# The first expert item picked by 0/1 matmuls, the last item combined by a matmul, the first norm taken over token rows, and the query and key norms packed in 16 rows

## The reference, cut to what matters

```
# layer 0
h = rmsnorm(x, norm_mix_even)                   # mean of squares over the 1024 channels of a token
a, gate, q, k, v = split(h @ w_in)
c = silu(layernorm(causal_depthwise_conv(a * sigmoid(gate))))     # 31 taps
q, k = rmsnorm(q per head of 64), rmsnorm(k per head of 64)       # 8 heads each
o = stick_breaking(q, k, v)                     # the samples also over 256 cached keys and values
x = x + concat(c, o) @ w_out;  x = x + swiglu(rmsnorm(x))
# layer 1
x = x + retention(rmsnorm(x))
h = rmsnorm(x, norm_ffn_odd)
top_val, top_idx = top_k(h @ router_w, 2);  gates = softmax(top_val)
x = x + sum over e of combine[:, e] * ((silu(h @ w_gate[e]) * (h @ w_up[e])) @ w_down[e])   # 8 experts, each token in 2
```

## Time and profile before

| | us |
|---|---|
| median of 3 runs (1799.4 to 1803.44) | 1800.45 |
| the profiled execution's own time | 1801.37 |
| its span in the trace | 1799.6 |
| PE busy | 1677.4 (93% of the span) |
| DVE busy | 1293.9 (72%) |
| ACT busy | 1049.5 (58%) |
| POOL busy | 71.2 (4%) |

### The profile page before, as it was taken

One profiled execution on the slowest core, in us unless ns is written; L12 is line 12 of the kernel. 1 busy time (PEld: TensorE's weight loads), 2 busy tenths in 40 slices (PEclk: granted clock), 3 DMA queues, 4 the chain that ended last, 5 costly groups with the idle time before them and its releaser, 6 DMA issues.

```text
span 1799.6 us, 24257 instructions
## 1 busy us (share of the span) xinstructions
PE 1677.4 (93%) x9295; PEld 1446.3 (80%) x9295; DVE 1293.9 (72%) x1091; ACT 1049.5 (58%) x913; POOL 71.2 (4%) x94
## 2 busy tenths in 40 slices
PE   4986989999899998939999999999999999999995
PEld 3964989999899987928878878878788788787884
DVE  4796255544964366348888888888888888888885
ACT  3534244433342265237787777777877877868773
POOL 2014000000001000010000000000000000000001
PEclk9998699999998799969999999999999999999998
DMA  6525049755557332639999999999999999999992
GB/s 232 193 74 166 1 135 371 254 176 176 186 189 249 126 106 82 223 131 365 369 351 395 364 357 386 351 378 379 351 393 363 359 392 357 360 383 354 386 368 98
DMA packets 236652, 491.69 MB, mean 273 GB/s; under 512 B 8665, under 2 KB 66137, under 8 KB 236328
## 3 DMA queue, kind: packets, MB, share of 16 engines
q1 hardware_dynamic: 227088, 456.60, 70.6%
q0 software_dynamic: 9504, 34.24, 5.8%
HBM read 463.87 MB, written 27.42 MB: 273 GB/s over the span
## 4 chain that ended last, share of the span: by engine, by line
issue 56%; PE 33%; DVE 7%; ACT 2%; DMA 1%; POOL 0%; POOLq 0%; SPq 0%; DVEq 0%; ACTq 0%
PE bank L624 8%; PE bank L625 8%; PE bank L626 8%; PE bank L910 2%; PE bank L847 1%; DVE WL L1482 1%; DVE even_CA L1541 1%; PE bank L744 1%; DVE RS L1556 1%; DMA R<-in_param 1%; PE bank L898 1%; ACT WH L1153 1%; PE bank L1006 1%; PE bank L981 0%; PE bank L884 0%
## 5 line engine op out<-in xcount | busy, mean ns | idle before, releaser
L1847 DVE TENSOR_TENSOR WL<-moe_MORE,WH 128x2048 fp32r<-128x2048 f32 x192 | 439.3, 2291 | 86.2 <-ACT WH L1410 85.7
L1410 ACT ACTIVATE WH<-moe_MORE 128x2048 fp32r<-128x2048 f32 x192 | 368.4, 1923 | 149.6 <-PE bank L626 149.5
L1847 DVE TENSOR_TENSOR WL<-ring,WH 128x2048 fp32r<-128x2048 f32 x144 | 329.2, 2291 | 56.8 <-ACT WH L1410 55.5
L624 PE MATMUL bank<-WH,moe_XEH 128*128 128x512 f32 x896 | 360.3, 402 | 3.0 <-DVE moe_XEL L1853 2.3
L626 PE MATMUL bank<-WH,moe_XEL 128*128 128x512 f32 x896 | 354.5, 396 | 0.0
L625 PE MATMUL bank<-WL,moe_XEH 128*128 128x512 f32 x896 | 354.3, 395 | 0.0
L1410 ACT ACTIVATE WH<-ring 128x2048 fp32r<-128x2048 f32 x144 | 275.9, 1919 | 85.4 <-PE bank L626 85.4
L624 PE MATMUL bank<-HH,WH 128*128 128x264 f32 x960 | 283.9, 296 | 19.3 <-DVE HL L1500 18.2
L1482 DVE TENSOR_TENSOR WL<-ring,WH 128x2048 fp32r<-128x2048 f32 x80 | 181.0, 2264 | 140.0 <-ACT WH L1153 139.8
L625 PE MATMUL bank<-HL,WH 128*128 128x264 f32 x960 | 278.7, 290 | 0.0
L626 PE MATMUL bank<-HH,WL 128*128 128x264 f32 x960 | 278.2, 290 | 0.0
(11 more groups left out here) (296 smaller groups left out, 1850.9 us busy)
## 6 DMA issues: line engine op xcount, KB each, us to landing
moe_MORE<-in_moe_w_gate SPq DMA_DIRECT2D x72, 1024.0 KB, 6.3
moe_MORE<-in_moe_w_up SPq DMA_DIRECT2D x72, 1024.0 KB, 6.5
ring<-in_moe_w_down SPq DMA_DIRECT2D x64, 1024.0 KB, 6.7
moe_MORE<-in_moe_w_down SPq DMA_DIRECT2D x48, 1024.0 KB, 5.8
ring<-in_moe_w_gate SPq DMA_DIRECT2D x40, 1024.0 KB, 5.6
ring<-in_moe_w_up SPq DMA_DIRECT2D x40, 1024.0 KB, 6.7
ring<-in_w_in_odd SPq DMA_DIRECT2D x24, 1024.0 KB, 5.4
ring<-in_ffn_w_gate SPq DMA_DIRECT2D x11, 1024.0 KB, 8.2
```

Of the source, the lines that this page charges most:

```text
L624: mm(out, lh, rh, start=start, stop=False)
L1410: func(WH[:, q % WRING, :], chunk(q), ACT.Copy).then_inc(s_hi, 1)
L1847: V.tensor_tensor(WL[:, q % WRING, :], chunk(q), full(WH[:, q % WRING, :]), ALU.subtract)\
```

## The change

Four parts, and the waits that go with them:

1. **Start.** The first 128 token rows and only the identity and epsilon of `C` are loaded first, then the other rows and `R`, then two chunks, then the rest of `C`. ACT squares the rows as they lie (a sum for each token), DVE multiplies each row by its reciprocal root (`XN`), PE turns these to channels, ACT takes gain and rounding in one step from PSUM and DVE the rest, and PE begins chunk 0. The turns of the plain rows for `XT` come behind chunk 0.
2. **Query and key norms.** Eight matmuls with a 0/1 table sum the squares of all 16 heads into 16 rows, between the projections; one root and one reciprocal of 16 x 264 follow, the latter inside DVE's convolution loop; `SPREAD`, made by POOL, brings each row back to its 64 partitions by a matmul, and DVE multiplies from PSUM.
3. **First item.** DVE writes 0/1 tables `OH` (token by slot); 24 matmuls of `HX` by them give the turned tile of item 0, without the trip through memory. Two weight chunks are split earlier on ACT and DVE, one inside the squares. ACT also keeps the residual as rows, `XR`.
4. **Last item.** It is not written. POOL gathers the rows of the other items while the last one is computed (a row of the last item is read as zero), multiplies them by the gates and adds them and `XR`: 12 TENSOR_TENSORs of 1024 columns. At the end PE multiplies `YE` by a table `GT` of gates, token by slot, and DVE adds. 4 small transfers to `moe_pad` fill up the count of a semaphore, and two more 512 KB tiles are zeroed in the feed-forward stage.

```
# SP, start
-            sp.dma_start(XI[:, 0:2, :], x_prompt.rearrange("o (a p) d -> p (o a) d", p=P)).then_inc(s_x, 16)
-            sp.dma_start(XI[0:NS, 2, :], x_sample.rearrange("b o d -> (b o) d")).then_inc(s_x, 16)
-            sp.dma_start(C[:], const).then_inc(s_const, 16)
-            sp.dma_start(R[:], param).then_inc(s_const, 16)
+            sp.dma_start(XI[:, 0, :], x_prompt[0, 0:P, :]).then_inc(s_x0, 16)
+            sp.dma_start(C[:, 0:P + 1], const[:, 0:P + 1]).then_inc(s_x0, 16)
+            sp.dma_start(XI[:, 1, :], x_prompt[0, P:SEQ, :]).then_inc(s_x, 16)
+            sp.dma_start(XI[0:NS, 2, :], x_sample.rearrange("b o d -> (b o) d")).then_inc(s_x, 16)
+            sp.dma_start(R[:], param).then_inc(s_x, 16)
+            load_in(q, w_in_even[0], starts[0])
+            load_in(q + 1, w_in_even[0], starts[1])
+            sp.dma_start(C[:, P + 1:NCONST], const[:, P + 1:NCONST]).then_inc(s_const, 16)
# DVE, query and key norms
             for n in range(2 * HP):
-                dve.wait_ge(s_qrt, n + 1)
-                link(V.reciprocal(RS[:, n % 2, :], RS[:, n % 2, :]))
+                dve.wait_ge(s_qms, n + 2)
                 V.scalar_tensor_tensor(out=QN[:, n, :], in0=QR[:, n, :], scalar=param_("q_g" if n < HP else "k_g"),
-                                       in1=RS[:, n % 2, :], op0=ALU.mult, op1=ALU.mult).then_inc(s_qn, 1)
+                                       in1=PB[6 + n % 2][:, 0:T], op0=ALU.mult, op1=ALU.mult).then_inc(s_qn, 1)
# PE, first item
+            pe.wait_ge(s_oh, 1)
+            pe.wait_ge(s_hx, 2 * NT)
+            for k in range(DK):
+                for t in range(NT):
+                    last = mm(PB[2 if k < 4 else 7][:, (k % 4) * P:(k % 4 + 1) * P],
+                              HX[0:TOK[t], t, k * P:(k + 1) * P], OH[0:TOK[t], t, :],
+                              start=(t == 0), stop=(t == NT - 1))
+            last.then_inc(s_xtp, 1)
-            pe.wait_ge(s_hx, 2 * NT)
-            turn_in(0)
# POOL, last item
-            pool.wait_ge(s_ylast, 16)
+            pool.wait_ge(s_last, 1)
+            pool.wait_ge(s_rows, 16 * 2 * NT)
+            pool.wait_ge(s_yst, N_FILL + 16 * (MAXI - 1))
...
+            for t in range(NT):
+                y0, y1 = YO[rows, t, :], SPARE[t][rows, :]
+                pool.wait_ge(s_gy[t], 32)
+                for c, y in enumerate((y0, y1)):
+                    nc.gpsimd.tensor_tensor(y, y, GE[rows, t, 2 + c:3 + c].to_broadcast([TOK[t], D]), ALU.mult)\
+                        .then_inc(s_pre, 1)
+                pool.wait_ge(s_pre, 4 * t + 2)
+                nc.gpsimd.tensor_tensor(y0, y0, y1, ALU.add).then_inc(s_pre, 1)
+                pool.wait_ge(s_pre, 4 * t + 3)
+                nc.gpsimd.tensor_tensor(y0, y0, XR[t][rows, :], ALU.add).then_inc(s_pre, 1)
# PE, end
+            for half in range(2):
+                pe.wait_ge(s_yee, n_items * 2 + (1 + half))
+                for t in range(NT):
+                    mm(PB[back_bank(half, t)][0:TOK[t], :], GT[:, t * P:t * P + TOK[t]],
+                       YE[:, half * 512:(half + 1) * 512], start=True, stop=True).then_inc(s_turn, 1)
```

More of the change, by code:

```diff
@@ L113, in build @@
         XT = sb("XT", [P, DK, T])
-        HH = sb("HH", [P, DK, T], F32R)
-        HL = sb("HL", [P, DK, T], F32R)
+        rows_at = -(-nc.sbuf_base // 32) * 32
+        sb("rows", [P, 2 * DK * T])
+        HH = nc.alloc_sbuf_tensor_at("HH", [P, DK, T], F32R, offset=rows_at)
+        HL = nc.alloc_sbuf_tensor_at("HL", [P, DK, T], F32R, offset=rows_at + 4 * DK * T)
+        SPARE = [nc.alloc_sbuf_tensor_at(f"SPARE{i}", [P, D], F32, offset=rows_at + 2 * i * DK * T) for i in range(4)]
         SQ = sb("SQ", [P, DK, T])
@@ L684, in down, with turn_tokens @@
                         q += 1
-            pe.wait_ge(s_x, 32)
-            pe.wait_ge(s_const, 32)
+            def turn_tokens(x, k):
+                for t in range(NT):
+                    last = turn(PB[4 + k % 4][:, t * P:t * P + TOK[t]],
+                                x[0:TOK[t], t, k * P:(k + 1) * P], ident[0:TOK[t], 0:TOK[t]])
+                last.then_inc(s_turn, 1)
+            pe.wait_ge(s_x0, 32)
+            pe.wait_ge(s_ht, NT)
+            for k in range(4):
+                turn_tokens(XN, k)
+            arrived(C_EVEN)
+            wh, wl = (as_in(x) for x in parts(C_EVEN))
+            for k in range(DK):
+                pe.wait_ge(s_hl, k + 1)
+                for j in range(2):
+                    cols = slice(j * P, (j + 1) * P)
+                    last = mm3(PB[j][:, 0:T], wh[:, k, cols], wl[:, k, cols], HH[:, k, :], HL[:, k, :],
+                               k == 0, k == DK - 1)
+                    if k == DK - 1:
+                        last.then_inc(s_ag, 1)
+                if k + 4 < DK:
+                    turn_tokens(XN, k + 4)
             for k in range(DK):
@@ L691, in _ @@
                     pe.wait_ge(s_xt, k - 3)
-                for t in range(NT):
-                    last = turn(PB[k % 4][:, t * P:t * P + TOK[t]],
-                                XI[0:TOK[t], t, k * P:(k + 1) * P], ident[0:TOK[t], 0:TOK[t]])
-                last.then_inc(s_turn, 1)
+                turn_tokens(XI, k)
+            pe.wait_ge(s_xt, DK)
             pe.wait_ge(s_cc, 32)
@@ L719, in _ @@
                 project(C_EVEN + 8 + n // 2, n % 2, PB[n][:, 0:T], s_vp)
+                if n == 0:
+                    pe.wait_ge(s_qks, 2 * HP)
+                    for i in range(2 * HP):
+                        last = mm(PB[6][0:2 * H, 0:T], heads[:, 2 * H - 2 - 2 * i:4 * H - 2 - 2 * i], SQ[:, i, :],
+                                  start=(i == 0), stop=(i == 2 * HP - 1))
+                    last.then_inc(s_qms, 1)
             pe.wait_ge(s_vfe, HP)
@@ L786, in _ @@
             pe.wait_ge(s_uo, 2)
[L787 removed]
+            pe.wait_ge(s_qn, 2 * HP)
             pe.wait_ge(s_qse, 1)
@@ L1824, in _ @@
             V.tensor_copy(DX[:, :], DF[:, :]).then_inc(s_dest, 1)
+            slots = PB[3][:, 0:P]
+            for t in range(NT):
+                last = V.tensor_scalar(OH[:, t, :], slots, DF[:, t:t + 1], None, ALU.is_equal)
+            link(last)
+            for t in range(NT):
+                last = V.scalar_tensor_tensor(out=OH[:, t, :], in0=slots, scalar=DF[:, NT + t:NT + t + 1],
+                                              in1=OH[:, t, :], op0=ALU.is_equal, op1=ALU.add)
+            last.then_inc(s_oh, 1)
             rows_hx(1)
```

295 lines of the change are left out of this document (188 added, 107 removed).

## The result

The changed kernel took 1793.41 us (median of 5, 1792.15 to 1794.62) against 1800.96 for the kernel before (5, 1799.4 to 1803.44): ratio 0.996, interval 0.9946 to 0.9975. It is 7.6 us faster, less than the forecast (1780) and outside its range (1763 to 1790). A second measurement of the same two kernels gave 1797.62 (12 executions, 1789.14 to 1804.0) against 1800.39, ratio 0.9985, 0.9966 to 1.0004.

What follows compares the result with a forecast made beforehand. TensorE was busy 93% of the span, so only PE's waits or slow stretches could be won. Terms: -8.0 - 2.0 - 11.2 - 13.4 + 14 = -20.6 us, giving 1780 for the median, range 1763 to 1790.

Steps and rivals of the forecast that it cites:

- A: Start: PE begins chunk 0 16.3 us earlier, less new turns and DVE work, a gain of 8.0 us (3.7 to 11).
- B: Query and key norms: one reciprocal in DVE's loop instead of eight behind it, a gain of 2.0 us (0.5 to 3.5).
- C: Head of the expert stage: item 0 picked by matmul begins 9.6 us earlier and at full clock, gain 11.2 us.
- D: End: from PE's last matmul to the span's end 9.8 us instead of 23.3, a gain of 13.4 us.
- E: Last item: POOL's 12 operations delay DVE's rests by 1.4 us each, a loss of 14 us (0 to 18).
- 21 passes slow and 27 fast, 8.3 us: Head of the expert stage: 48 gather passes, slow ones at 0.24 us and fast ones at 0.12, 8.3 us in all.
- Item 0 at full clock: Head of the expert stage: item 0 starts at full clock, saving the 1.7 us its first ten matmuls lost.
- all passes slow: Head of the expert stage, lower bound: the passes take 11.5 us and item 0 loses again, gain 6.3 us.
- the eight matmuls lie in projections for which DVE's loop leaves room: Norms: the eight 0/1 matmuls are hidden in the projections; without DVE's loop they would cost 1.9 us.
- the 1.5 given back: Last item: DVE's operations that read PSUM can lie beside POOL, taking about 1.5 us off a loss of 15.5.
- the first rival: Last item: POOL's operations cost nothing, total gain 34.6 us, time 1766; chance 0.19.
- the second rival: Start: chunk 0 lands at 23.6 as before, so the start gives 0.4 us, time 1788; chance 0.14.

Runs made afterwards that it cites:

- e9: Changed kernel with its first item again loaded through memory, without 0/1 tables and their matmuls: 1796.01 us, ratio 0.9973 to the kernel before.
- e5: Changed kernel with the norms of queries and keys done as before, for each tile: 1798.25 us, ratio 0.9992 to the kernel before.
- f2: Changed kernel with the three edits of f1 plus the old norms (e5) and the unread matmuls (e3): 1768.48 us, ratio 0.9817 to the kernel before.
- e2: Changed kernel with the root behind the projections and the reciprocal at the end of DVE's convolution loop: 1800.02 us, ratio 0.9991 to the kernel before.
- e4: Changed kernel with POOL's early copy and first cached keys held until weight chunk 0 has landed: 1791.82 us, ratio 0.9949 to the kernel before.
- f1: Changed kernel with the edits of e4, e6 and e7 together: 1771.0 us, ratio 0.9848 to the kernel before.
- e1: Changed kernel without POOL's twelve products and sums, its six gathers kept: 1778.89 us, ratio 0.9884 to the kernel before.
- e7: Changed kernel with POOL's twelve operations replaced by six of DVE in the last item: 1778.65 us, ratio 0.9883 to the kernel before.
- e8: Changed kernel whose twelve POOL operations cover 512 of the 1024 columns: 1782.81 us, ratio 0.9903 to the kernel before.
- e3: Changed kernel with 28 extra unread PE matmuls of 384 columns ahead of the gather: 1791.86 us, ratio 0.9953 to the kernel before.
- e6: Changed kernel with the first item's gather turned round, 512 columns of rows passing a stationary 0/1 table: 1791.47 us, ratio 0.9953 to the kernel before.

## Why the prediction was wrong, step by step

The forecast was 20.6 us, the first profile gives 7.9. By its own terms:

| part | forecast | measured | |
|---|---|---|---|
| A, start | -8.0 | -5.3 | chunk 0 at 19.5, taken as 16 |
| B, norms | -2.0 | +1.9 | the sums in the projections |
| C, first item | -11.2 | -2.7 | 0.31 us a pass, clock never back |
| D, end | -13.4 | -13.4 | 9.9 us, forecast 9.8 |
| E, last item | +14 | +15.7 | right mechanism |
| clock of the odd layer | 0 | -4.8 | 3.4 fortune, 1.4 open |
| slow drift over the items | 0 | +0.7 | 0.5 to 0.7 in all thirteen profiles, not explained |

**C failed most, by 8.5 us.** The step is "21 passes slow and 27 fast, 8.3 us". I took the time at half clock that chunk 0 showed, with matmuls of 264 columns, and used it for passes of 128 columns. All 48 ran slow, 15.0 us, and a slow pass took 0.31, not 0.24, which was the row of turns. "Item 0 at full clock" fell with it: its first matmuls lost 2.5 us where they had lost 1.7. The text had a bound for "all passes slow", 6.3; the measured 2.7 lies outside even that, through the dearer pass. The small steps were near: `HX` 0.6 late for 1.4, the tables 1.7 for 1.3. e9 adds what neither the forecast nor a rival had: with the earlier splits alone, the way through memory gained 3.0 as well.

**B failed by 3.9 us**, in "the eight matmuls lie in projections for which DVE's loop leaves room". PE had no room: it ran one projection behind another, and 16 passes of 0.23 (priced at 0.12) stood in the chain, 3.73 us in the row of L783. The other half was right: from the end of the projections (1.4 ahead, by 98.17 for the next turns before and 96.76 now) to the keys' turns (3.35 ahead) the gain is 1.95, forecast 2.0, the first of the three convolutions at half clock as forecast (5.86). That it came so near is luck in part: the forecast's own terms from 112 add up to 126.8 and not 126.0, a gain of 1.3, and a pair of spreads took 1.1 and not 0.5, which an earlier begin made good. e5, f2 and e2 show the failed half: without the packing the loss in the projections is gone, with a late root it stays.

**A is a size.** The mechanism was as told (rows first, chunk last, turns inside it). Chunk 0 landed at 19.5, inside the bounds of 13 and 20.3, but not near the first. In the ten profiles with POOL's early queue ACT began to copy it between 16.9 and 21.5, in the three without (e4, f1, f2) at 13.4 or before: what held it was POOL's queue. e4 brings the gain to 9.8.

**E was right in its mechanism, 1.7 short.** Twelve operations at 1.3 each; without the 1.5 given back for DVE's operations that read PSUM, the forecast's sum is 15.5; e1, e7 and e8 tell it from the gathers, from the clock and from a fixed price. POOL free, the first rival, did not come; the second rival's time (1788) was nearer the result than the forecast, for another reason. **D** came to the tenth.

The range ended at 1790 since the lower bounds of A, B and C were never put together: A at 3.7, B at 0.5 and C at 6.3 with E at 18 and D as it is leave 5.9 us, 1794.6. B and C came out beyond their worst ends, and E near its own.

## What to carry to other kernels

Work that is moved under a stage where PE is never idle is free only if it does not hold up the engines that feed PE: POOL's 12 operations, each of which kept DVE waiting, cost 15.7 us there, and the same sums in six operations of DVE's own 0.5. A matmul put into a chain that has no gap delays all behind it, whatever it saves elsewhere; look for PE's own gap before calling it hidden. Before a transfer is replaced by arithmetic, look at what is queued ahead of it: here the memory path with earlier splits gained as much (3.0 against 2.7).

## What the runs showed of the hardware

The granted clock at the head, one profile each. In the changed kernel it was half through all 48 passes of 128 columns, 15 us without a gap, and rose at 793.1, in item 0. In e3 the same passes began at full clock after a wait of 2.64 us, and it was half from 771.1, 2 us later. With 12 passes of 512 columns it rose 9 us after they began in e6 and 4 us after in f1; in f2, where they began at full clock after a wait of 2.63 us, it was full through them all. In the waits of 2.2 to 3.0 us that followed, it fell to half again (e6, f1, f2).

POOL and DVE excluded each other also where DVE had a single tensor in SBUF, the product with one scalar for each row in e3: 5.42 us instead of 0.74, its end 0.55 behind the end of POOL's second product. The Trainium skill ("SBUF — State Buffer", section "Who interferes with whom") names such an operation among those that can take the shared ports, and says that whoever holds them blocks the other for the whole instruction; the trace agrees, and an operation that reads PSUM beside one in SBUF (L2019, 0.67) was not held.

Executions of one kernel on one chip differ by up to 15 us (1789.14 to 1804.0), and where the two profiles of the changed kernel differ, most of that lies in one stretch of half clock in the odd layer. What sets its place was not tried.
